# Expert routing rewritten: pairwise comparisons, unnormalised exponentials, ranks summed in PSUM, places in two halves

## Chip, cores and metric

The kernel runs on one core of one Trainium2 chip. The metric is the device time of one execution in microseconds; lower is better.

## What is computed

Two decoder layers over 512 tokens of width 1024. Layer 0 mixes tokens by sliding-window attention with sinks, layer 1 by forgetting attention. Each mixer is followed by a layer norm, a mixture of experts and another layer norm. The part that matters here is the router of the mixture of experts, which both layers share:

```python
def grouped_moe(h, w_router, b_router, w_gate, w_up, w_down):
    logits = (h2 @ w_router).astype(jnp.float32) + b_router.astype(jnp.float32)
    scores = jax.nn.softmax(logits, axis=-1)
    g = scores.reshape(T, N_GROUPS, EXPERTS_PER_GROUP)        # 4 groups of 4 experts
    group_score = jnp.sum(lax.top_k(g, TOP_K)[0], axis=-1)    # sum of the two best
    best = jnp.argmax(group_score, axis=-1)
    in_group = jax.nn.one_hot(best, N_GROUPS, dtype=jnp.bool_)[:, :, None]
    masked = jnp.where(in_group, g, -1.0).reshape(T, N_EXPERTS)
    top_vals, top_idx = lax.top_k(masked, TOP_K)              # two experts of that group
    gates = top_vals / jnp.sum(top_vals, axis=-1, keepdims=True)
    ...
    hg = jnp.einsum('td,edf->tef', h2, w_gate)
    hu = jnp.einsum('td,edf->tef', h2, w_up)
    act = jax.nn.silu(hg) * hu * gate_dense[:, :, None].astype(h2.dtype)
    y = jnp.einsum('tef,efd->td', act, w_down)
```

Each token uses two experts of one group, with gates that sum to 1.

## The kernel before

Every engine has a program written out by hand, with semaphores between them; there is no scheduler. Tokens lie in NT = 4 tiles of 128 on the partitions. The helper `link` puts a semaphore on a VectorE instruction and makes the next one wait for it, since a later instruction on the same engine may otherwise start before the result is written.

In a layer, the stages are: input projection, attention, output projection with the first norm (four token tiles, each followed by `route(t)`, the router's matmuls L648 into bank 7), the routing, the expert loop, the sum of each token's two expert rows with the second norm. The residual state goes to DRAM (`xd`) on ScalarE's queue as soon as a tile is normed (L909).

**The routing** (VectorE, L1248 to L1330) works on tiles of 128 partitions with 4 token tiles x 16 experts = 64 columns. It adds the bias and subtracts the maximum (L1251 to L1253), ScalarE takes the exponential (L913), and then VectorE

- sums and divides (L1255 to L1257);
- forms the six pair sums of every group, whose maximum is the group's score (L1259 to L1262);
- finds the best group, ties going to the first, through a maximum, an equality, a product with falling numbers `w4`, and a second maximum and equality (L1263 to L1268);
- masks the other groups (L1270 to L1273) and finds the best expert and the second in the same way with `w16` (the loop L1274 to L1282): one-hot tiles `oh1` and `oh2`;
- writes their sum `asn_b` in bf16 (L1283), which TensorE waits for;
- prepares `id_part`, one-hot times token number in fp16 (L1286), and the gates (L1287 to L1290);
- waits for the ranks. TensorE has multiplied `asn_b` by a strictly triangular matrix (`before_b`, L674: how many tokens earlier in the tile chose the expert) and by ones (L675: the tile's count). VectorE copies both from PSUM, forms running totals over the tiles and adds them (L1293 to L1297);
- picks each token's rank at its two experts (L1298, L1299) and compares it with the CAP = 96 places (`place_is`, L1300, 768 columns).

TensorE then multiplies `place_is` by `id_part` (L680, eight matmuls): the result is, for each expert and place, the token number. VectorE casts it into `row_ids` (L1303), and POOL gathers the rows of each expert from `xd` with an indirect DMA (L429), four experts ahead (experts 0 to 3 at once). What VectorE does after that (L1305 to L1329: overflow of an expert beyond 96 tokens, and `pos`, the place where each token's rows will be found) is needed at the end of the expert loop.

**The expert loop.** For expert e, TensorE turns the gathered rows (`turn_rows`, L687), ScalarE copies them as the high part (L925), VectorE forms the low part (L1336), and TensorE runs gate and up in three products per tile (L491 to L493). Meanwhile ScalarE and VectorE split the next expert's weights (L904, L1222). The down product is L713. SP loads the weights through a ring of four slots. The loads for experts 0 to 3 are issued from the end of the output projection on; from expert 4 on each waits for `gu_done` or `y_done` of the expert four back.

Of the kernel before, what the change touches and what calls it, by code (L numbers as in the profile page):

```python
# [48 lines left out]
def trunk(nc, x, ln_gain, ln_bias, swa_w_in, swa_sinks, swa_w_o, fox_w_in, fox_b_f, fox_w_o,  # L49
# [8 lines left out]
    with ctx:  # L58
# [77 lines left out]
        red = small(SM + 640, 10, NT)  # L136
        ids = small(SM + 684, OVF + 1)
# [4 lines left out]
        w4 = sb("w4", [P, NG])  # L142
        w16 = sb("w16", [P, NE])
# [105 lines left out]
        def _(eng):  # L249
# [33 lines left out]
            for l, (w_in, w_o) in enumerate(((swa_w_in[0], swa_w_o[0]), (fox_w_in[0], fox_w_o[0]))):  # L283
# [40 lines left out]
                eng.wait_ge(S(f"routed{l}"), 1)  # L324
# [18 lines left out]
        def _(eng):  # L343
# [16 lines left out]
            link(eng.iota(w4[:, :], [[-1, NG]], base=NG, channel_multiplier=0, allow_small_or_imprecise_dtypes=True))  # L360
            link(eng.iota(w16[:, :], [[-1, NE]], base=NE, channel_multiplier=0, allow_small_or_imprecise_dtypes=True))
# [104 lines left out]
        def _(eng):  # L466
# [16 lines left out]
            for l in range(DEPTH):  # L483
# [158 lines left out]
                def route(t):  # L642
# [7 lines left out]
                    mm.then_inc(S(f"logits{l}"), 1)  # L650
# [66 lines left out]
                def step(i, u, first=False, last=False):  # L717
# [5 lines left out]
                    if not first:  # L723
                        eng.wait_ge(S(f"h_ready{l}"), e)
                        turn_h((u - 1) % 2).then_inc(S(f"hT_done{l}"), 1)
# [7 lines left out]
                def down_of(e, b, use, loaded, reused):  # L733
                    eng.wait_ge(S(f"d_loaded{use % RING}"), loaded)
                    eng.wait_ge(S(f"hT_ready{l}"), e + 1)
                    if reused:
                        eng.wait_ge(S(f"y_act{l}"), e)
                        eng.wait_ge(S(f"y_dve{l}"), e)
# [12 lines left out]
                eng.wait_ge(S(f"h_ready{l}"), NE)  # L751
                turn_h(1).then_inc(S(f"hT_done{l}"), 1)
# [3 lines left out]
                with eng.If(n_ovf > 0):  # L756
                    eng.wait_ge(S(f"y_act{l}"), NE)
                    eng.wait_ge(S(f"y_dve{l}"), NE)
# [13 lines left out]
        def _(eng):  # L772
# [32 lines left out]
            for l in range(DEPTH):  # L805
# [111 lines left out]
                def store_rows(e, b):  # L917
                    eng.wait_ge(S(f"y_dve{l}"), e + 1)
                    eng.wait_ge(S(f"y_act{l}"), e + 1)
# [9 lines left out]
                def silu(e, b):  # L929
                    eng.wait_ge(S(f"gu_done{l}"), e + 1)  # L930
                    eng.activation(ssb[0:CAP, b, :], bank[2 + b][0:CAP, 0:F], ACT.Silu).then_inc(S(f"silu{l}"), 1)
# [528 lines left out]
```

## Time and profile before

| | us |
|---|---|
| median of 3 runs | 988.99 (987.59 to 992.05) |
| the profiled execution | 988.5 |
| its span in the profile | 986.6 |
| PE busy | 829.8 (84%) |
| VectorE busy | 547.7 (56%) |
| ScalarE busy | 383.9 (39%) |
| POOL busy | 136.1 (14%) |
| share of the chain that ended last: PE, DVE, DMA | 81%, 9%, 4% |

The profile is one execution, recorded by the hardware. "Span" is from its first to its last instruction; the execution's own time is 1.9 us longer. PE is TensorE's matmuls, PEld its weight loads, DVE VectorE, ACT ScalarE, POOL GpSimd, SP the engine that issues most DMAs. Busy shares are averages over stages with different limits, so what a change in one stage is worth has to be read in that stage.

### The profile page before, as it was taken

The page shows a single profiled execution, that of the slowest core. Times are in us where ns is not written, and L with a number is a line of the kernel's source. Part 1 is how long each engine was busy: PE and PEld are TensorE (multiplying, and loading weights), DVE is VectorE, ACT ScalarE, POOL GpSimd, SP SyncE. Part 2 cuts the span into 40 slices and gives each one's busy share as a digit, 9 for nine tenths or more (in the row PEclk, how much of TensorE's full clock was granted, in tenths as well). Part 3 has the DMA queues.
Part 4 walks back from the last instruction along what each step waited for, and adds up shares of the span by engine and source line. Part 5 has one row for each costly group of instructions (what it writes and reads, how often), then busy time and mean ns, then how long its engine had stood idle before and what let it go on. Part 6 is the DMA issues. An engine that isn't in the chain of part 4 may idle for free.

```text
span 986.6 us, 11641 instructions
## 1 busy us (share of the span) xinstructions
PE 829.8 (84%) x4140; PEld 601.7 (61%) x4140; DVE 547.7 (56%) x1086; ACT 383.9 (39%) x763; POOL 136.1 (14%) x153
## 2 busy tenths in 40 slices
PE   6999999981989999818999999999981889999910
PEld 4887777871546565417878877887861556556500
DVE  4534884556557676366332225664556556767437
ACT  4323884002455555231222226775001365555300
POOL 2000221121001000032000002221111100100033
PEclk9999999985899999959999999999985799999965
DMA  9942000149699998645062223111139599999144
GB/s 320 349 138 86 2 1 1 43 170 336 189 353 332 360 353 316 219 141 183 30 215 86 86 86 107 65 44 44 43 119 360 151 340 340 361 357 374 42 124 158
DMA packets 106851, 183.11 MB, mean 186 GB/s; under 512 B 6496, under 2 KB 72032, under 8 KB 106800
## 3 DMA queue, kind: packets, MB, share of 16 engines
q1 hardware_dynamic: 92864, 132.34, 39.7%
q0 software_dynamic: 9200, 33.33, 10.9%
q10 hardware_dynamic: 4736, 16.78, 4.5%
q8 instruction: 29, 0.48, 0.2%
q14 instruction: 22, 0.18, 0.1%
HBM read 159.60 MB, written 22.84 MB: 185 GB/s over the span
## 4 chain that ended last, share of the span: by engine, by line
PE 81%; DVE 9%; DMA 4%; issue 3%; POOL 2%; ACT 1%; POOLq 0%; DVEq 0%; SPq 0%; ACTq 0%
PE bank L491 16%; PE bank L492 16%; PE bank L493 16%; PE bank L713 12%; PE bank L613 5%; PE bank L579 4%; PE bank L596 3%; PE bank L687 2%; PE bank L477 2%; DMA arena<-xd,row_ids 1%; PE bank L648 1%; POOL veps L387 1%; DVE xres L1042 1%; DMA arena<-ys,pos 1%; PE bank L621 1%
## 5 line engine op out<-in xcount | busy, mean ns | idle before, releaser
L1222 DVE TENSOR_TENSOR low<-ring,gu_high 128x1024 fp32r<-128x1024 f32 x128 | 151.2, 1221 | 50.6 <-ACT gu_high L904 50.6
L904 ACT CAST gu_high<-ring 128x1024 fp32r<-128x1024 f32 x128 | 127.7, 1049 | 16.8 <-DVE arena L1353 16.8
L713 PE MATMUL bank<-ring,arena 128*96 128x512 f32 x256 | 119.8, 611 | 11.3 <-issue 9.2
L491 PE MATMUL bank<-gu_high,rows_high 128*96 128x512 f32 x256 | 115.4, 451 | 8.2 <-DVE rows_low L1336 8.2
L492 PE MATMUL bank<-low,rows_high 128*96 128x512 f32 x256 | 103.6, 405 | 0.0
L493 PE MATMUL bank<-gu_high,rows_low 128*96 128x512 f32 x256 | 103.0, 402 | 0.0
L713 PEld LDWEIGHTS bank<-ring,arena 128*96 128x96 f32 x256 | 40.1, 167 | 67.7 <-issue 67.3
L852 ACT ACTIVATE arena<-arena,nmax 128x256 f32<-128x256 f32 (+3 forms) x128 | 66.8, 522 | 30.8 <-DVE nmax L1153 20.0
L491 PE MATMUL bank<-high,x_high 128*128 128x512 f32 x160 | 66.2, 414 | 10.3 <-DVE low L1048 5.1
L414 POOL TENSOR_TENSOR low<-ring,high 128x512 fp32r<-128x512 f32 x32 | 40.6, 1269 | 231.1 <-ACT high L872 231.1
L613 PE MATMUL bank<-arena 128*128 128x64 f32 x544 | 68.1, 269 | 0.2 <-ACT arena L866 0.2
L613 PEld LDWEIGHTS bank<-arena 128*128 128x128 f32 x544 | 65.8, 192 | 0.5 <-ACT arena L866 0.5
L429 POOL DMA_INDIRECT arena<-xd,row_ids x32 | 30.2, 944 | 258.2 <-PE bank L687 220.0
L492 PE MATMUL bank<-low,x_high 128*128 128x512 f32 x160 | 64.7, 404 | 0.0
L493 PE MATMUL bank<-high,xlow 128*128 128x512 f32 x160 | 64.6, 404 | 0.0
L491 PEld LDWEIGHTS bank<-gu_high,rows_high 128*96 128x96 f32 x256 | 42.9, 167 | 33.3 <-DVE rows_low L1336 9.1
L492 PEld LDWEIGHTS bank<-low,rows_high 128*96 128x96 f32 x256 | 42.7, 167 | 23.7 <-issue 7.9
L493 PEld LDWEIGHTS bank<-gu_high,rows_low 128*96 128x96 f32 x256 | 42.7, 167 | 19.2 <-issue 0.9
L491 PE MATMUL bank<-high,attn_high 128*128 128x512 f32 x128 | 51.5, 402 | 0.0
L493 PE MATMUL bank<-high,attn_low 128*128 128x512 f32 x128 | 51.3, 401 | 0.0
L491 PE MATMUL bank<-x_high,wsplit 128*128 128x512 f32 x128 | 50.8, 397 | 0.0
L492 PE MATMUL bank<-xlow,wsplit 128*128 128x512 f32 x128 | 50.8, 397 | 0.0
(207 smaller groups left out, 1399.2 us busy)
## 6 DMA issues: line engine op xcount, KB each, us to landing
ring<-in_w_gate SPq DMA_DIRECT2D x32, 1024.0 KB, 12.3
ring<-in_w_up SPq DMA_DIRECT2D x32, 1024.0 KB, 14.4
ring<-in_w_down SPq DMA_DIRECT2D x32, 1024.0 KB, 12.7
ys<-arena ACTq DMA_DIRECT2D x32, 384.0 KB
ring<-in_fox_w_in SPq DMA_DIRECT2D x6, 2048.0 KB, 10.7
ring<-in_swa_w_in SPq DMA_DIRECT2D x3, 2048.0 KB, 8.8
ring<-in_swa_w_o SPq DMA_DIRECT2D x2, 2048.0 KB, 17.4
xd<-xres ACTq DMA_DIRECT2D x8, 512.0 KB, 2.6
```

The costliest lines, as they stand in the source:

```text
L414: eng.tensor_tensor(low, w, high, ALU.subtract).then_inc(S(f"out_low{l}"), 1)
L429: eng.indirect_dma_start(xe[0:CAP, e % RING, :], None, xd, bass.IndirectOffsetOnAxis(ap=row_ids[:, e:e + 1], axis=0)).then_inc(S(f"xe_in{l ...
L491: eng.matmul(out, ah, wh, start=(c == 0), stop=False)
L492: eng.matmul(out, ah, wl, start=False, stop=False)
L493: return eng.matmul(out, al, wh, start=False, stop=(c == KC - 1))
L579: mm = eng.matmul(s_bank(s, half)[:, 0:nk], QT[r, hp, n * P:(n + 1) * P], KT[r, kp, k0 * P:k1 * P], start=True, stop=(l == 0))
L596: mm = eng.transpose(bank[3 + half][:, i * P:(i + 1) * P], sp[:, 2 * (s % 2) + half, i * P:(i + 1) * P], ident[:, :])
L613: mm = eng.matmul(bank[5 + hp % 2][:, at:at + HD], pT[:, half, i * P:(i + 1) * P], (V0 if l == 0 else V)[:, k0 + i, v:v + HD], start=(i == ...
L713: mm = eng.matmul(bank[5 + half][0:CAP, :], hT[:, b, c, :], w[:, c, half * BLK:(half + 1) * BLK], start=(c == 0), stop=(c == FC - 1))
L852: eng.activation(p, p, ACT.Exp, bias=nmax[:, hp % 2, n, half:half + 1], scale=-1.0, accum_out=rsum[:, hp % 2, n, half:half + 1]).then_inc( ...
L904: eng.copy(gu_high[u % 2][:, part, :], slot_in(use)[:, part, :]).then_inc(S("gu_high"), 1)
L1222: eng.tensor_tensor(lows[use % RING][:, part, :], slot_in(use)[:, part, :], gu_high[u % 2][:, part, :], ALU.subtract).then_inc(S("gu_low"), 1)
```

## The change

- The exponentials are no longer divided by their sum. The gates are a ratio, and all comparisons are inside a token, so the common factor drops out.
- The best group: each group's score is compared with the score of each group (16 differences per token), a difference must reach `lead`, which is 0 or 1e-30 depending on which of the two comes first, and the minimum over the row says whether a group wins against all (`gk`).
- The scores of the best group's four experts are collected into `best` (product with `gk` in the turned order, then a sum). Again each is compared with each, and the number of wins (4: first, 3: second) gives `top`, `won` and from them `asn_b`, `oh1` and `oh2`.
- TensorE sums the ranks over the tiles in PSUM: tile t of bank 2 gets `before_b` times its own tile and `ones_b` times each earlier tile (10 matmuls of 16 columns), and the total of each expert goes to bank 6 (4 matmuls). VectorE's running totals go away; it reads the ranks in PSUM directly.
- `place_is` is written in two halves of 384 columns, and TensorE's wait for it is split the same way.
- The gates and the copies of ranks and counts move behind `row_ids`. One product of the gates, `won` times `best`, stands between `place_is` and the wait for `ids_done`.
- On POOL at the start, the iotas of `w4` and `w16` become a memset and a select for `lead`.
- Many semaphores that had one name per layer (`routed`, `logits`, `hT_done`, `h_ready`, `hT_ready`, `y_act`, `y_dve`, `silu`) now have one for both layers, with the wait counts raised by NE or NT in layer 1; who waits for whom stays.

The core of the diff:

```diff
                 eng.wait_ge(S("assigned"), l + 1)
-                eng.matmul(bank[2][:, 0:NT * NE], before_b[:, :], asn_b[:, :], start=True, stop=True)
-                eng.matmul(bank[6][:, 0:NT * NE], ones_b[:, :], asn_b[:, :], start=True, stop=True).then_inc(S("ranked"), 1)
-
-                eng.wait_ge(S("places_ready"), l + 1)
+                for t in range(NT):
+                    for u in range(t + 1):
+                        mm = eng.matmul(bank[2][:, t * NE:(t + 1) * NE], before_b[:, :] if u == t else ones_b[:, :],
+                                        asn_b[:, u * NE:(u + 1) * NE], start=(u == 0), stop=(u == t))
+                mm.then_inc(S("ranked"), 1)
+                for t in range(NT):
+                    mm = eng.matmul(bank[6][:, 0:NE], ones_b[:, :], asn_b[:, t * NE:(t + 1) * NE], start=(t == 0), stop=(t == NT - 1))
+                mm.then_inc(S("counted"), 1)
+
                 for k in range(TOPK):
+                    eng.wait_ge(S("places_ready"), TOPK * l + k + 1)
                     for t in range(NT):
...
                 eng.wait_ge(S("expd"), l + 1)
-                link(eng.tensor_reduce(sm, pr, X, ALU.add))
-                link(eng.reciprocal(rs, sm))
-                link(eng.tensor_tensor(pr, pr, over(rs, NE), ALU.mult))
...
                 link(eng.tensor_reduce(gs, pair, X, ALU.max))
-                link(eng.tensor_reduce(gm, gs, X, ALU.max))
-                link(eng.tensor_tensor(gk, gs, over(gm, NG), ALU.is_equal))
-                link(eng.tensor_tensor(gk, gk, tiles(w4[:, :]), ALU.mult))
-                link(eng.tensor_reduce(kb, gk, X, ALU.max))
-                link(eng.tensor_tensor(gk, gk, over(kb, NG), ALU.is_equal))
...
-                for v, kk, oh in ((v1, k1, oh1), (v2, k2, oh2)):
-                    link(eng.tensor_reduce(v, msk, X, ALU.max))
-                    link(eng.tensor_tensor(tmp, msk, over(v, NE), ALU.is_equal))
-                    link(eng.tensor_tensor(tmp, tmp, tiles(w16[:, :]), ALU.mult))
-                    link(eng.tensor_reduce(kk, tmp, X, ALU.max))
-                    link(eng.tensor_tensor(oh, tmp, over(kk, NE), ALU.is_equal))
...
+                link(eng.tensor_tensor(square, *against(gs), ALU.subtract))
+                link(eng.tensor_tensor(square, square, leads, ALU.is_ge))
+                link(eng.tensor_reduce(gk, square, X, ALU.min))
+
+                by_place = tmp.rearrange("p t (e g) -> p t e g", g=NG)
+                link(eng.tensor_tensor(by_place, prg.rearrange("p t g e -> p t e g"), against(gk)[1], ALU.mult))
+                link(eng.tensor_reduce(best, by_place, X, ALU.add))
+
+                link(eng.tensor_tensor(square, *against(best), ALU.subtract))
+                link(eng.tensor_tensor(square, square, leads, ALU.is_ge))
+                link(eng.tensor_reduce(wins, square, X, ALU.add))
+                link(eng.tensor_scalar(top, wins, EPG - 1.5, None, ALU.is_ge))
+                eng.tensor_tensor(asn_b[:, :].rearrange("p (t g e) -> p t g e", t=NT, g=NG), against(top)[1], against(gk)[0], ALU.mult).then_inc(S("assigned"), 1)
+                eng.tensor_scalar(won[:, 0, :, :], wins, float(EPG), None, ALU.is_equal)
+                link(eng.tensor_scalar(won[:, 1, :, :], wins, EPG - 1.0, None, ALU.is_equal))
+                for k, oh in enumerate((oh1, oh2)):
+                    ins = eng.tensor_tensor(oh.rearrange("p t (g e) -> p t g e", g=NG), against(won[:, k, :, :])[1], against(gk)[0], ALU.mult)
+                link(ins)
...
+                eng.wait_ge(S("ranked"), l + 1)
+                lranks = bank[2][:, 0:NT * NE].rearrange("p (t e) -> p t e", t=NT)
+                link(eng.tensor_tensor(lp12, oh12, lranks.unsqueeze(1).to_broadcast([P, 2, NT, NE]), ALU.mult))
+                link(eng.tensor_reduce(rank[:, :, :], lp12, X, ALU.add))
+                for k in range(TOPK):
+                    eng.tensor_tensor(place_is[:, k, :, :], places[:, :].unsqueeze(1).to_broadcast([P, NT, CAP]),
+                                      rank[:, k, :].unsqueeze(2).to_broadcast([P, NT, CAP]), ALU.is_equal).then_inc(S("places_ready"), 1)
+                eng.tensor_tensor(won, won, best.unsqueeze(1).to_broadcast([P, 2, NT, EPG]), ALU.mult).then_inc(S("dve_won"), 1)
+                eng.wait_ge(S("ids_done"), l + 1)
+                eng.tensor_copy(row_ids[:, :], bank[5][0:CAP, 0:NE]).then_inc(S("ids_ready"), 1)
+                eng.wait_ge(S("dve_won"), l + 1)
+                eng.tensor_reduce(v1, won[:, 0, :, :], X, ALU.add)
+                link(eng.tensor_reduce(v2, won[:, 1, :, :], X, ALU.add))
```

The order of instructions is the order in the code. VectorE, layer 0, from the reduction of the pair sums; in the kernel before the piece shown ends at the first maximum of the expert search, 12 instructions ahead of `asn_b` (`arena` holds all the small tiles, `w` is `w4` or `w16`):

```order
L1262 TENSOR_REDUCE arena<-arena 128x16
L1263 TENSOR_REDUCE arena<-arena 128x4
L1265 TENSOR_TENSOR arena<-arena 128x16
L1266 TENSOR_TENSOR arena<-arena,w 128x16
L1267 TENSOR_REDUCE arena<-arena 128x4
L1268 TENSOR_TENSOR arena<-arena 128x16
L1270 TENSOR_SCALAR arena<-arena 128x16
L1272 TENSOR_TENSOR arena<-arena 128x64
L1273 TENSOR_TENSOR arena<-arena 128x64
L1275 TENSOR_REDUCE arena<-arena 128x4
```

The same place with the change, up to `asn_b`:

```order
L1270 TENSOR_REDUCE arena<-arena 128x16
L1278 TENSOR_TENSOR arena<-arena 128x64
L1279 TENSOR_TENSOR arena<-arena,lead 128x64
L1280 TENSOR_REDUCE arena<-arena 128x16
L1283 TENSOR_TENSOR arena<-arena 128x64
L1284 TENSOR_REDUCE arena<-arena 128x16
L1286 TENSOR_TENSOR arena<-arena 128x64
L1287 TENSOR_TENSOR arena<-arena,lead 128x64
L1288 TENSOR_REDUCE arena<-arena 128x16
L1289 TENSOR_SCALAR arena<-arena 128x16
L1290 TENSOR_TENSOR asn_b<-arena 128x64
```

The search for the best group has become three instructions, and `asn_b` follows after five more on the four collected scores and one threshold.

VectorE, layer 0, from the arrival of the ranks to the cast of the row numbers, before:

```order
L1293 COPY arena<-bank 128x64
L1294 COPY arena<-bank 128x64
L1296 TENSOR_TENSOR arena<-arena 128x16 x3
L1297 TENSOR_TENSOR arena<-arena 128x48
L1298 TENSOR_TENSOR arena<-arena 128x128
L1299 TENSOR_REDUCE arena<-arena 128x8
L1300 TENSOR_TENSOR place_is<-places,arena 128x768
L1303 CAST row_ids<-bank 96x16
```

With the change, from the instruction behind `asn_b` (`bank` is the rank tile in PSUM):

```order
L1291 TENSOR_SCALAR arena<-arena 128x16
L1292 TENSOR_SCALAR arena<-arena 128x16
L1294 TENSOR_TENSOR arena<-arena 128x64 x2
L1298 TENSOR_TENSOR id_part<-arena,tok_id 128x128
L1302 TENSOR_TENSOR arena<-arena,bank 128x128
L1303 TENSOR_REDUCE arena<-arena 128x8
L1305 TENSOR_TENSOR place_is<-places,arena 128x384 x2
L1307 TENSOR_TENSOR arena<-arena 128x32
L1309 CAST row_ids<-bank 96x16
```

The copies and running totals ahead of the masked ranks are gone, the one-hot tiles come ahead of them instead, and the places are two instructions.

TensorE, layer 0, from the ranks to the turning of expert 0's rows, before:

```order
L648 MATMUL bank7<-wr,xT 128x16 x8
L674 MATMUL bank2<-asn_b,before_b 128x64
L675 MATMUL bank6<-asn_b,ones_b 128x64
L680 MATMUL bank5<-id_part_59,place_is_58 96x16 x8
L687 MATMUL bank0<-ident,arena 128x96 x4
```

With the change:

```order
L681 MATMUL bank2<-asn_b,before_b 128x16
L681 MATMUL bank2<-asn_b,ones_b 128x16
L681 MATMUL bank2<-asn_b,before_b 128x16
L681 MATMUL bank2<-asn_b,ones_b 128x16 x2
L681 MATMUL bank2<-asn_b,before_b 128x16
L681 MATMUL bank2<-asn_b,ones_b 128x16 x3
L681 MATMUL bank2<-asn_b,before_b 128x16
L685 MATMUL bank6<-asn_b,ones_b 128x16 x4
L691 MATMUL bank5<-id_part_59,place_is_58 96x16 x8
L698 MATMUL bank0<-ident,arena 128x96 x4
```

One matmul of 64 columns has become ten of 16 ahead of the signal `ranked`, and the counts come behind it.

## Rows read from the trace of the kernel before

**Rows 1.** The page, chain that ended last, shares of the span by engine

```profile
PE 81%; DVE 9%; DMA 4%; issue 3%; POOL 2%; ACT 1%; POOLq 0%; DVEq 0%; SPq 0%; ACTq 0%
```

**Rows 2.** Chain in order of time, both layers' first gather: start us, us, what

```profile
235.31 6.25 DMA arena<-xd,row_ids
...
241.60 1.55 PE bank L687 x8
...
244.14 1.03 DVE rows_low L1336 x2
...
756.36 8.06 DMA arena<-xd,row_ids
```

**Rows 3.** Timeline of VectorE, layer 0, routing: start us, us, line, shapes

```profile
223.19 0.22 DVE L1255 TENSOR_REDUCE arena<-arena 128x4 f32<-128x64 f32 x1 [0.32 <-ACT arena L913]
...
223.92 0.21 DVE L1259 TENSOR_TENSOR arena<-arena 128x48 f32<-128x48 f32 x1
...
224.36 0.25 DVE L1262 TENSOR_REDUCE arena<-arena 128x16 f32<-128x96 f32 x1
224.65 0.17 DVE L1263 TENSOR_REDUCE arena<-arena 128x4 f32<-128x16 f32 x1
...
225.68 0.17 DVE L1270 TENSOR_SCALAR arena<-arena 128x16 f32<-128x16 f32 x1
225.89 0.22 DVE L1272 TENSOR_TENSOR arena<-arena 128x64 f32<-128x64 f32 x1
226.15 0.22 DVE L1273 TENSOR_TENSOR arena<-arena 128x64 f32<-128x64 f32 x1
...
229.47 0.23 DVE L1283 TENSOR_TENSOR asn_b<-arena 128x64 bf16<-128x64 f32 x1
229.61 0.28 DVE L1286 TENSOR_TENSOR id_part<-arena,tok_id 128x128 f16<-128x128 f32 x1
229.81 0.15 DVE L1287 TENSOR_TENSOR arena<-arena 128x4 f32<-128x4 f32 x1
...
230.49 0.22 DVE L1293 COPY arena<-bank 128x64 f32<-128x64 f32 x1
...
231.75 0.29 DVE L1298 TENSOR_TENSOR arena<-arena 128x128 f32<-128x128 f32 x1
...
232.39 0.96 DVE L1300 TENSOR_TENSOR place_is<-places,arena 128x768 f16<-128x768 f32 x1
234.25 0.17 DVE L1303 CAST row_ids<-bank 96x16 uint32<-96x16 f32 x1 [0.90 <-PE bank L680]
...
239.79 0.17 DVE L1329 CAST ovf_id<-arena 1x11 int32<-1x11 f32 x1
```

**Rows 4.** Timeline of VectorE, layer 1, routing

```profile
744.29 0.22 DVE L1255 TENSOR_REDUCE arena<-arena 128x4 f32<-128x64 f32 x1 [0.32 <-ACT arena L913]
...
755.36 0.17 DVE L1303 CAST row_ids<-bank 96x16 uint32<-96x16 f32 x1 [0.90 <-PE bank L680]
```

**Rows 5.** Timeline of TensorE in the routing; last row: line L680, min/median/max ns

```profile
229.75 0.24 PE L674 MATMUL bank<-asn_b,before_b 128*128 128x64 bf16 x1 [7.66 <-DVE asn_b L1283]
229.76 0.12 PEld L675 LDWEIGHTS bank<-asn_b,ones_b 128*128 128x128 bf16 x1
...
233.40 0.81 PE L680 MATMUL bank<-id_part,place_is 128*96 128x16 f16 x8 [3.36 <-DVE place_is L1300]
...
L680 PE MATMUL bank<-id_part,place_is x16: 227/228/248, 233.4 to 755.1; 128*96 128x16 f16 x16
```

**Rows 6.** Windows, all engines, layer 0: busy us, PE clock, DMA share, GB/s

```profile
225.00:230.00 5.00, 0.25 (x2) 0.13 (x2) 4.32 (x22) 0.98 (x2) 0.00 (x0) 0.50 1.06 388
...
240.00:245.00 5.00, 1.54 (x8) 1.25 (x8) 0.86 (x2) 1.80 (x3) 0.91 (x1) 0.50 0.92 234
245.00:250.00 5.00, 4.78 (x12) 3.22 (x13) 3.57 (x4) 0.34 (x1) 0.00 (x0) 0.52 0.29 83
```

**Rows 7.** Line L429, the gathers: issue to landing, those the view could pair

```profile
DMA to landing us min/median/max: 6.7/7.8/9.1
```

More of the change, by code:

```diff
@@ L136, in trunk @@
         red = small(SM + 640, 10, NT)
+        best = small(SM + 816, NT, EPG)
+        wins = small(SM + 832, NT, EPG)
+        won = small(SM + 848, 2, NT, EPG)
+        top = small(SM + 880, NT, EPG)
         ids = small(SM + 684, OVF + 1)
@@ L359, in _ @@
                                    base=0, pattern=[[-1, P]], channel_multiplier=1))
-            link(eng.iota(w4[:, :], [[-1, NG]], base=NG, channel_multiplier=0, allow_small_or_imprecise_dtypes=True))
-            link(eng.iota(w16[:, :], [[-1, NE]], base=NE, channel_multiplier=0, allow_small_or_imprecise_dtypes=True))
+            link(eng.memset(lead[:, :, :], 0.0))
+            link(eng.affine_select(out=lead[:, :, :], in_=lead[:, :, :], compare_op=ALU.is_ge, fill=1e-30,
+                                   base=0, pattern=[[-1, NG], [1, EPG]], channel_multiplier=0))
             link(eng.iota(e_cap[:, :], [[CAP, NE]], base=0, channel_multiplier=0, allow_small_or_imprecise_dtypes=True))
@@ L1246, in tiles @@
                     return a.unsqueeze(1).to_broadcast([P, NT, a.shape[1]])
-                mx, sm, rs, gm, kb, v1, k1, v2, k2 = (red[:, k, :] for k in range(9))
-                eng.wait_ge(S(f"logits{l}"), NT)
+                mx, sm, rs, v1, v2 = (red[:, k, :] for k in range(5))
+                eng.wait_ge(S("logits"), NT + NT * l)
                 lps = bank[7][:, 0:NT * NE].rearrange("p (t e) -> p t e", t=NT)
@@ L1290, in _ @@
                 link(eng.tensor_tensor(gates[:, :, 1], v2, rs, ALU.mult))
-                eng.wait_ge(S("ranked"), l + 1)
-                eng.tensor_copy(tmp, bank[2][:, 0:NT * NE].rearrange("p (t e) -> p t e", t=NT))
-                link(eng.tensor_copy(tot, bank[6][:, 0:NT * NE].rearrange("p (t e) -> p t e", t=NT)))
-                for t in range(1, NT):
-                    link(eng.tensor_tensor(tot[:, t, :], tot[:, t, :], tot[:, t - 1, :], ALU.add))
-                link(eng.tensor_tensor(tmp[:, 1:NT, :], tmp[:, 1:NT, :], tot[:, 0:NT - 1, :], ALU.add))
-                link(eng.tensor_tensor(lp12, oh12, tmp.unsqueeze(1).to_broadcast([P, 2, NT, NE]), ALU.mult))
-                link(eng.tensor_reduce(rank[:, :, :], lp12, X, ALU.add))
-                eng.tensor_tensor(place_is[:, :, :, :], places[:, :].unsqueeze(1).unsqueeze(1).to_broadcast([P, 2, NT, CAP]),
-                                  rank[:, :, :].unsqueeze(3).to_broadcast([P, 2, NT, CAP]), ALU.is_equal).then_inc(S("places_ready"), 1)
-                eng.wait_ge(S("ids_done"), l + 1)
-                eng.tensor_copy(row_ids[:, :], bank[5][0:CAP, 0:NE]).then_inc(S("ids_ready"), 1)
+                eng.wait_ge(S("counted"), l + 1)
+                eng.tensor_copy(tmp, lranks)
+                link(eng.tensor_copy(tot[:, NT - 1, :], bank[6][:, 0:NE]))
                 cnt = tot[:, NT - 1, :]
```

59 lines of the change are left out of this document (27 added, 32 removed).

## The prediction

> **What bounds the kernel now.** I read the page's chain of waits first. It puts 81% of the span on TensorE and 9% on VectorE [rows 1], so I looked for the places where VectorE is on the chain. The chain in order of time shows them: in each layer, between the router's logits and the first expert, TensorE has next to nothing to do and waits for a serial piece of VectorE work, then for the gather of expert 0's rows [rows 2]. In layer 0 the gather starts at 235.31 and takes 6.25 us; in layer 1 it starts at 756.36 and takes 8.06 us. Behind it follow the turning of the rows (241.60), VectorE's low parts (244.14) and the experts.
>
> The timeline of VectorE shows the serial piece [rows 3]: from L1255 (223.19) to the start of the row numbers' cast L1303 (234.25) are 11.06 us, nearly all of it instructions of 0.15 to 0.3 us, each waiting for the one before. Layer 1 has the same piece: 744.29 to 755.36, 11.07 us [rows 4]. Nothing hides it, because gather, TensorE and ScalarE's L925 all stand behind it. So a microsecond off this piece is a microsecond off the span, twice, unless the gather gives it back. TensorE's part is small: the two rank matmuls wait for L1283 and start at 229.75, the eight L680 take 0.81 us [rows 5].
>
> **What the change does, per layer.** I cost by distance from start to start, since that holds the link's wait too.
>
> *Up to asn_b.* Before: 223.19 to 229.47, 6.28 us. Now the first instruction after the exponentials is the pair sum. The three pair sums up to L1262 take 0.44 (223.92 to 224.36), the reduction of pairs 0.29 (224.36 to 224.65). Then come eight 64-wide linked steps (difference, comparison, reduction, masked product, reduction, difference, comparison, count); such a step takes 0.26 (225.89 to 226.15). A 16-wide scalar step (top) takes 0.21 (225.68 to 225.89). Sum 0.44 + 0.29 + 8 x 0.26 + 0.21 = 3.02, so 3.26 less. No row before reads a 64-wide tile in the turned order that by_place uses; between 0.21 and 0.29 for each of the eight steps the sum is 2.6 to 3.3. I take 0.26, because L1272 already reads with broadcast strides at that price.
>
> *asn_b to the masked ranks.* Before: 229.47 to 231.75 (L1298), 2.28 us, with the gates' arithmetic, two copies out of PSUM and the running totals in it. Now VectorE needs 0.14 (229.47 to 229.61, the step of an instruction that the next need not wait for), 0.14 and 0.21 for won, 0.14 and 0.26 for the two one-hot tiles, 0.20 for id_part (229.61 to 229.81): 1.09. But it then waits for ten matmuls where there was one on that path. TensorE starts 0.28 after asn_b's start (229.75 less 229.47). L680 gives 0.81 for eight with 96-wide weights and 0.23 for one, so 0.083 for each further one; with 128-wide weights 0.083 x 128 / 96 = 0.11. That makes 0.28 + 9 x 0.11 + 0.24 + 0.02 = 1.53 us, so the matmuls are late, not VectorE. Ends: 1.28 (0.083 each) and 1.65 (0.12, the weight load of L675). Gain 0.75. The four "counted" matmuls behind (0.44) end before place_is is there. The masked ranks now read PSUM themselves. The 64-wide copy out of PSUM, L1293, took 0.22 us and 64-wide operations inside SBUF 0.22 to 0.23 [rows 3], so I add nothing. The Trainium skill ("VectorE: DVE Perf Modes", the section on the TRN2 errata) gives PSUM sources a fixed part 62 cycles longer, which would be 0.06 us per layer; the rows do not show it.
>
> *The places.* L1298 to L1300 stays at 0.64. From L1300 to L1303 were 1.86: 0.96 for 768 columns, eight matmuls 0.81, 0.09 for signals. With (0.96 - 0.28) / 640 = 1.06 ns a column (L1286 has 128 columns at 0.28), a half of 384 takes 0.55 and lets the second start after 0.47 (asn_b, 0.23 long, let the next start after 0.14, some 0.08 ahead of its end). The second half ends at 1.02, four matmuls then take 0.81 - 4 x 0.083 = 0.48, with signals 1.59. Gain 0.27; the ends are 0 (the halves overlap with nothing) and 0.4.
>
> *Sum per layer*: 3.26 + 0.75 + 0.27 = 4.28 us, ends 3.6 and 4.8.
>
> *What moves behind the row numbers.* won times best (one 32-wide step, 0.2) stands ahead of the wait for ids_done, while TensorE still works at the second half. Behind L1303 go the gates and two copies, some 1.4 us. VectorE was done 5.7 us after L1303 began (234.25 to 239.96) and is next wanted at 244.14 [rows 2, 3], so 7.1 us of work lie under 9.9 us. Cost nothing; if the gather took over 2.8 us less, this tail would be what is late next. The two iotas become a memset and a select on POOL at the start, long before use. The merged semaphores add some additions on registers in layer 1's loops on PE, ACT and DVE, in front of waits; the matmuls of the loop show no gap at the ones that are there. Nothing.
>
> **What the gather gives back.** Its issue moves from 235.31 to about 231.0. There the DMA engines are fuller: at 225 to 230 their share is 1.06 with 388 GB/s, at 240 to 245 it is 0.92 with 234 GB/s, and at 245 to 250 only 0.29 [rows 6]. The weight loads of experts 0 to 3 run until about then. Layer 0's 6.25 us had the end of this burst; issued earlier, it has the full stream, as the gathers in the expert loop do. Those land in 6.7 to 9.1 us, median 7.8 [rows 7]. I take 7.8 for both layers: +1.55 in layer 0, -0.26 in layer 1, together +1.3.
>
> **Sum.** 988.5 (the profiled execution's own time; the median of the runs is 989.0) - 2 x 4.28 + 1.3 = **981.2 us**, 0.8% less. The experts and the second layer shift with it: their loads are released by TensorE's own progress.
>
> **Rivals.**
> 1. *The gather ends with the burst whenever it is issued.* For it: both first gathers landed (241.56, 764.42) near the end of the burst, and the rate drops behind. Then the 4.28 us are spent waiting: **988.5**. Against it: in the loop gathers land in 7.8 us under a stream that does not end. The Trainium skill ("DMA: Bandwidth & Descriptors", Queues, rings and completion order) says that a DMA's completion is written only after all earlier writes of that DMA engine, over all its queues; by that rule the gather would wait for the weights already in flight, and the loop's 7.8 us bound how much. Chance 0.09.
> 2. *The gather is not slowed at all.* 6.25 us in both layers: 988.5 - 8.6 - 1.8 = **978.1**. For it: layer 0's 6.25 was under a nearly full stream too (0.92 at 240 to 245). Against: layer 1, the same place, took 8.06. Chance 0.10.
> 3. *Slower: the four gathers share.* POOL issues gathers 0 to 3 one after another. If rows of all four go out side by side under the full stream, gather 0 completes only with the last of them, at the end of the burst: by 245 in layer 0 [rows 6], by 766.1 in layer 1, whose routing stands 521.1 later [rows 3, 4]. That is 3.4 and 1.7 later than now, **993.6**. It decides from a landing of 10.5 us on (6.25 + 4.28), where the gain of layer 0 is gone; no landing that the view gives is above 9.1 [rows 7]. Chance 0.03.
>
> A last uncertainty is TensorE's clock. It was at the lower level (1.2 GHz, 0.50) while TensorE waited and on the mean still at 0.52 at 245 to 250, with TensorE busy again for 4.78 of 5 us [rows 6]. How long the low stretch lasts after the restart can come out otherwise when the start shifts: I allow 1 us in all, either way.
>
> **How the numbers follow.** The forecast's case (landings of 7.1 to 9.1, mean near 7.8) has 0.78. Its ends: -9.6 - 1.8 - 1 gives 976.1 and -7.2 + 3.9 (both at 9.1) + 1 gives 986.2; I give **976.5 to 986.0**, which leaves out rivals 1 and 3 and little else, some 15%. Half a percent, about what a measurement of this kernel can tell, is 4.9 us: faster means under 984.1, slower over 993.9. Of the forecast's case 0.07 lies above 984.1, so faster 0.71 + 0.10 = 0.81; same 0.07 + 0.09 + 0.01 = 0.17; slower 0.02, the part of rival 3 that a lost microsecond or two of clock pushes over.
>
> **What would show it.** The distance from ScalarE's exponential to the row numbers' cast should be 6.5 to 7.3 us instead of 11.06, in both layers. asn_b should start about 3.0 after the first pair sum, and the masked ranks about 1.5 after asn_b, with VectorE waiting for the rank matmuls. The gather of expert 0 should take 7 to 9 us in layer 0. Wrong would be: a gather over 9 us (rival 1 or 3), VectorE late for L1336, or turned reads well over 0.26 us a step.

## Result and profile after

The kernel with the change takes 982.72 us in the median of 7 runs (980.65 to 983.39), the kernel before 990.42 us (7 runs, 987.59 to 993.27): ratio 0.9918, 95% interval 0.99 to 0.9936. The forecast was 981.2 us in a range of 976.5 to 986.0. The profiled execution of the changed kernel took 981.84 us, that of the kernel before 988.5.

The page of the changed kernel, its span and the shares of its chain:

```profile
span 980.1 us, 11701 instructions
...
PE 82%; DVE 8%; DMA 4%; issue 3%; POOL 2%; ACT 1%; POOLq 0%; SPq 0%; DVEq 0%; ACTq 0%
```

The span is 6.5 us shorter than before (986.6), VectorE's share of the chain one point smaller [rows 1]. VectorE in layer 0's routing and, last two rows, in layer 1's (start, duration, instruction):

```profile
223.02 0.21 DVE L1267 TENSOR_TENSOR arena<-arena 128x48 f32<-128x48 f32 x1 [0.32 <-ACT arena L924]
...
223.47 0.25 DVE L1270 TENSOR_REDUCE arena<-arena 128x16 f32<-128x96 f32 x1
223.75 0.22 DVE L1278 TENSOR_TENSOR arena<-arena 128x64 f32<-128x64 f32 x1
...
224.52 0.26 DVE L1283 TENSOR_TENSOR arena<-arena 128x64 f32<-128x64 f32 x1
224.82 0.22 DVE L1284 TENSOR_REDUCE arena<-arena 128x16 f32<-128x64 f32 x1
...
226.05 0.22 DVE L1290 TENSOR_TENSOR asn_b<-arena 128x64 bf16<-128x64 f32 x1
...
227.08 0.28 DVE L1302 TENSOR_TENSOR arena<-arena,bank 128x128 f32<-128x128 f32 x1
...
227.72 1.03 DVE L1305 TENSOR_TENSOR place_is<-places,arena 128x384 f16<-128x384 f32 x2
...
229.32 0.17 DVE L1309 CAST row_ids<-bank 96x16 uint32<-96x16 f32 x1 [0.48 <-PE bank L691]
...
236.10 0.16 DVE L1345 CAST ovf_id<-arena 1x11 int32<-1x11 f32 x1
...
740.91 0.21 DVE L1267 TENSOR_TENSOR arena<-arena 128x48 f32<-128x48 f32 x1 [0.32 <-ACT arena L924]
...
747.22 0.17 DVE L1309 CAST row_ids<-bank 96x16 uint32<-96x16 f32 x1 [0.48 <-PE bank L691]
```

From the first instruction after the exponentials to the row numbers' cast: 223.02 to 229.32, 6.30 us, where 11.06 stood [rows 3]; in layer 1 740.91 to 747.22, 6.31 us [rows 4]. That is 4.76 us less, twice; I had 4.28. TensorE in the same stretch, with `[idle before]` at the ends:

```profile
226.33 0.19 PE L681 MATMUL bank<-asn_b,before_b 128*128 128x16 bf16 x1 [4.41 <-DVE asn_b L1290]
...
226.62 0.25 PE L685 MATMUL bank<-asn_b,ones_b 128*128 128x16 bf16 x4
228.33 0.96 PE L691 MATMUL bank<-id_part,place_is 128*96 128x16 f16 x8 [1.45 <-DVE place_is L1305]
```

The rank matmuls start 0.28 us after `asn_b` and those ahead of `ranked` are spread over 0.3 us; `place_is` is what TensorE waits for. The chain from the gathers on, both layers:

```profile
230.39 7.99 DMA arena<-xd,row_ids
...
238.42 1.55 PE bank L698 x8
...
240.96 1.03 DVE rows_low L1352 x2
...
748.23 7.41 DMA arena<-xd,row_ids
```

Against [rows 2]: the gather in layer 0 takes 7.99 us instead of 6.25, the one in layer 1 7.41 instead of 8.06. Together 1.09 us of the gain is given back there. VectorE's work behind the row numbers ended at 236.26, 4.7 us before it was wanted at 240.96.

How the 6.5 us come about, each figure the difference of the same event in the two traces (after less before):

| event | after | before | difference |
|---|---|---|---|
| layer 0, first instruction after the exponentials | 223.02 | 223.19 | -0.17 |
| row numbers cast | 229.32 | 234.25 | -4.93 |
| expert 0's first gate/up matmul | 242.03 | 245.22 | -3.19 |
| layer 1, first instruction after the exponentials | 740.91 | 744.29 | -3.38 |
| row numbers cast | 747.22 | 755.36 | -8.14 |
| expert 0's first gate/up matmul | 759.29 | 768.09 | -8.80 |
| last down product | 928.66 | 936.33 | -7.67 |
| end of span | 980.1 | 986.6 | -6.5 |

By its restart, the first gate/up matmul of expert 0, layer 1 had won 8.8 us, of which 2.3 are gone at the end. Windows of 10 us from that restart, before and after (columns as in [rows 6]):

```profile
768.09:778.09 10.00, 8.26 (x32) 5.66 (x32) 4.58 (x6) 2.21 (x6) 0.90 (x1) 0.80 0.20 59
```

```profile
759.29:769.29 10.00, 9.05 (x32) 6.14 (x32) 3.79 (x5) 1.42 (x5) 0.67 (x1) 0.72 0.59 157
```

TensorE's mean granted clock is 0.72 instead of 0.80. In the single matmuls the lower level (one matmul every 0.43 us, 1.2 GHz) lasted 5.67 us after the restart instead of 3.95; in layer 0 it lasted 4.27 instead of 4.72. The expert loop of layer 1 is 1.1 us longer, and 0.8 of that is there already when the rows of expert 1 are turned (8.23 us behind the restart instead of 7.44). Another 1.0 us is the last store of expert rows, in the chain of the kernel before and of this one:

```profile
940.73 2.99 DMA ys<-arena
```

```profile
933.06 3.96 DMA ys<-arena
```

### The profile page after: what moved, and what is told of

Read it like the earlier page. It is cut to its first block, busy times and chain, and to the rows that moved or that the text cites. A ratio compares the mean times of both kernels' runs of the same rounds, so it can differ in the third digit from the quotient of the medians.

```text
span 980.1 us, 11701 instructions
## 1 busy us (share of the span) xinstructions
PE 831.0 (85%) x4164; PEld 602.4 (61%) x4164; DVE 542.4 (55%) x1066; ACT 384.2 (39%) x763; POOL 136.4 (14%) x153
## 4 chain that ended last, share of the span: by engine, by line
PE 82%; DVE 8%; DMA 4%; issue 3%; POOL 2%; ACT 1%; POOLq 0%; SPq 0%; DVEq 0%; ACTq 0%
PE bank L496 17%; PE bank L497 16%; PE bank L498 16%; PE bank L724 12%; PE bank L618 5%; PE bank L584 4%; PE bank L601 3%; PE bank L698 2%; PE bank L482 2%; DMA arena<-xd,row_ids 2%; PE bank L653 1%; DMA arena<-ys,pos 1%; POOL veps L392 1%; DVE xres L1053 1%; DVE stats L1038 1%
```

## Experiments

"Behind the exponentials" is below the distance from VectorE's first instruction after them to the cast of the row numbers, 11.06 us before and 6.30 after the change. Timed kernels come with a ratio to the kernel before in the same session.

**Only the comparisons.** The changed kernel with two rank matmuls and totals on VectorE, `place_is` in one piece, and the gates ahead of the ranks:

```diff
-                for t in range(NT):
-                    for u in range(t + 1):
-                        mm = eng.matmul(bank[2][:, t * NE:(t + 1) * NE], before_b[:, :] if u == t else ones_b[:, :],
...
+                eng.matmul(bank[2][:, 0:NT * NE], before_b[:, :], asn_b[:, :], start=True, stop=True)
+                eng.matmul(bank[6][:, 0:NT * NE], ones_b[:, :], asn_b[:, :], start=True, stop=True).then_inc(S("ranked"), 1)
...
+                link(eng.tensor_tensor(won, won, best.unsqueeze(1).to_broadcast([P, 2, NT, EPG]), ALU.mult))
+                eng.tensor_reduce(v1, won[:, 0, :, :], X, ALU.add)
+                link(eng.tensor_reduce(v2, won[:, 1, :, :], X, ALU.add))
...
+                eng.tensor_tensor(place_is[:, :, :, :], places[:, :].unsqueeze(1).unsqueeze(1).to_broadcast([P, 2, NT, CAP]),
...
```

> Only the comparisons and the unnormalised exponentials; ranks, places and the position of the gates as before. My theory (VectorE's steps are worth their length, twice): from the first instruction after the exponentials to the cast of the row numbers 8.8 us instead of 11.06 (3.0 to asn_b, then 2.0 with the gates in it, 1.26 of copies and totals, 0.64, 1.86), and the gather lands after 7 to 8 us, so 4.5 us less minus about 1 = 987 against 990.4. Rival (the gather ends with the burst of weight loads whenever it is issued): the same 8.8 us, but a landing longer by the 2.3 us won in each layer, and the time of before, 990.4.

Measured: 989.45 us, ratio 0.9981 (0.9967 to 0.9994), so only 2 us less than before. Behind the exponentials 9.02 us (222.85 to 231.87), 2.04 less. Up to `asn_b` it is 3.2 us less, but from there to the masked ranks it takes 3.47 us instead of 2.28, because the one-hot tiles, which stood ahead of `asn_b` before, now come behind it with `won`, and the gates have seven instructions instead of four. The chain:

```profile
232.93 8.69 DMA arena<-xd,row_ids
...
753.80 8.42 DMA arena<-xd,row_ids
```

The gather in layer 0 was issued 2.38 us earlier than before (232.93 against 235.31) and landed at 241.62, where it had landed at 241.56, so all of it was given back. In layer 1 it took 8.42 against 8.06 and gave back 0.36 of 2.07. The rival wanted both layers and the time of before, and falls. Nor does layer 0 show its mechanism, a gather that ends with the burst. In four of the kernels below that gather is issued 1.2 to 2.1 us earlier, takes 8.60 to 8.77 us there too, and lands earlier (239.46 to 240.50). In the changed kernel it landed at 238.38, while the last weight load of the burst, issued at 227.97, took 20.3 us, until 248.3. So layer 0 gave back all it had because the gather of the kernel before had 6.25 us, and one that is issued a little earlier has some 8.7.

**Ranks as before**, all else changed: the two rank matmuls above, and on VectorE

```diff
-                link(eng.tensor_tensor(lp12, oh12, lranks.unsqueeze(1).to_broadcast([P, 2, NT, NE]), ALU.mult))
+                eng.tensor_copy(tmp, bank[2][:, 0:NT * NE].rearrange("p (t e) -> p t e", t=NT))
+                link(eng.tensor_copy(tot, bank[6][:, 0:NT * NE].rearrange("p (t e) -> p t e", t=NT)))
+                for t in range(1, NT):
+                    link(eng.tensor_tensor(tot[:, t, :], tot[:, t, :], tot[:, t - 1, :], ALU.add))
+                link(eng.tensor_tensor(tmp[:, 1:NT, :], tmp[:, 1:NT, :], tot[:, 0:NT - 1, :], ALU.add))
+                link(eng.tensor_tensor(lp12, oh12, tmp.unsqueeze(1).to_broadcast([P, 2, NT, NE]), ALU.mult))
...
```

> The changed kernel with the ranks as before: two matmuls of 64 columns, both copies out of PSUM and the running totals. In the changed kernel the masked ranks start 1.03 us after asn_b. Theory now: this part is worth the 1.26 us of copies and totals in full, because ten narrow matmuls of 128-wide bf16 weights take only some 0.3 us; masked ranks 2.3 us after asn_b, span of the routing 7.56 instead of 6.30 us, 2 to 3 us more in all. Rival (my prediction's sizing): ten matmuls cost 0.5 us of it, so the part is worth 0.75 us per layer and the masked ranks come 1.8 us after asn_b.

VectorE in layer 0:

```profile
226.17 0.23 DVE L1284 TENSOR_TENSOR asn_b<-arena 128x64 bf16<-128x64 f32 x1
...
228.45 0.29 DVE L1300 TENSOR_TENSOR arena<-arena 128x128 f32<-128x128 f32 x1
```

`asn_b` to the masked ranks is 2.28 us against 1.03 in the changed kernel: 1.25, as the theory had it, not my 0.75. One run gave 988.5 us. The gathers took 8.60 and 8.46 us here, 1.7 us more in all than in the changed kernel. With 2 x 1.25 that makes 4.2 of the 5.8 us between the two. The trace places another 1.7 us where the two kernels are the same, between layer 0's last down product and layer 1's routing. Most of it is in the output projection of layer 1, whose first eight matmuls come 0.43 us apart (679.95 to 683.44), the lower clock level, and 0.23 us apart in the changed kernel. Seven of the twelve variants have such a slow projection in their traces, the kernel before and the changed kernel do not.

**`place_is` in one piece**, all else changed:

```diff
+                eng.wait_ge(S("places_ready"), l + 1)
                 for k in range(TOPK):
-                    eng.wait_ge(S("places_ready"), TOPK * l + k + 1)
...
-                for k in range(TOPK):
-                    eng.tensor_tensor(place_is[:, k, :, :], places[:, :].unsqueeze(1).to_broadcast([P, NT, CAP]),
...
+                eng.tensor_tensor(place_is[:, :, :, :], places[:, :].unsqueeze(1).unsqueeze(1).to_broadcast([P, 2, NT, CAP]),
+                                  rank[:, :, :].unsqueeze(3).to_broadcast([P, 2, NT, CAP]), ALU.is_equal).then_inc(S("places_ready"), 1)
```

> The changed kernel with place_is in one piece. Theory: place_is to row_ids 1.86 us instead of 1.60, so 0.26 us more per layer, 0.5 in all, below what the times can tell. Rival (the halves hide nothing, since TensorE's second half waits for VectorE anyway): 1.60 to 1.65 us here too.

```profile
227.17 0.96 DVE L1304 TENSOR_TENSOR place_is<-places,arena 128x768 f16<-128x768 f32 x1
...
229.03 0.17 DVE L1308 CAST row_ids<-bank 96x16 uint32<-96x16 f32 x1 [0.80 <-PE bank L691]
```

1.86 us from `place_is` to the row numbers against 1.60: the halves are worth 0.26 us per layer. The one run took 984.4 us, which says nothing about half a microsecond.

**The gates ahead of the ranks**, all else changed:

```diff
+                link(eng.tensor_tensor(won, won, best.unsqueeze(1).to_broadcast([P, 2, NT, EPG]), ALU.mult))
+                eng.tensor_reduce(v1, won[:, 0, :, :], X, ALU.add)
+                link(eng.tensor_reduce(v2, won[:, 1, :, :], X, ALU.add))
+                link(eng.tensor_tensor(sm, v1, v2, ALU.add))
+                link(eng.reciprocal(rs, sm))
+                eng.tensor_tensor(gates[:, :, 0], v1, rs, ALU.mult)
+                link(eng.tensor_tensor(gates[:, :, 1], v2, rs, ALU.mult))

                 eng.wait_ge(S("ranked"), l + 1)
...
```

> The changed kernel with the gates' arithmetic back ahead of the wait for the ranks (seven small instructions). Theory: rank matmuls are done long before VectorE gets there (1.03 us behind asn_b), so VectorE's 1.0 us of gates is paid in full: masked ranks 2.0 us behind asn_b, 1.0 us more per layer. Rival (the gates hide under the wait for the ten matmuls, as my sizing of 1.53 us had it): masked ranks at 1.5 us, half of it hidden.

```profile
226.21 0.23 DVE L1290 TENSOR_TENSOR asn_b<-arena 128x64 bf16<-128x64 f32 x1
...
228.42 0.29 DVE L1309 TENSOR_TENSOR arena<-arena,bank 128x128 f32<-128x128 f32 x1
```

From `asn_b` to the masked ranks 2.21 us instead of 1.03: 1.18 us, nothing of it hidden. Moving the gates behind the row numbers is thus nearly as large a part of the gain as the ranks in PSUM. The four parts add up to the whole: 2.04 for the comparisons, 1.25 for the ranks, 1.18 for the gates and 0.26 for the halves make 4.73 of the 4.76 us. The one run took 988.84 us; 2 x 1.18 and gathers that were 1.9 us longer (8.77 and 8.50) make 4.2 of its distance of 6.1, and this trace too has the slow projection in layer 1 and 1.7 us more between the same two places.

**Loads held.** To see what makes the gather slow, SP holds what is left of the burst:

```diff
                     if u >= OUT_BLOCKS:
                         load_gate_up(k, l, u, S(f"w_loaded{k % RING}"))
+                    if u == OUT_BLOCKS:
+                        eng.wait_ge(S(f"xe_in{l}0"), 16)
                     load_down(k, l, u, S(f"d_loaded{k % RING}"))
```

> The changed kernel, but SP holds the down weights of expert 2 and all loads of expert 3 until the gather of expert 0 has landed. Theory (the gather is slow because it shares the DMA engines with the burst of weight loads): it lands in 3 to 4 us instead of 8.0 and 7.4, expert 0 starts some 4 us earlier in each layer, 974 to 976 us. Rival 1 (the gather's own work, index reading and descriptors on POOL, is the 6 to 8 us): landing unchanged, 982. Rival 2 (held loads come late): landing 3 to 4 us, but ScalarE waits for the weights of expert 3 at its split, and the time is 982 or above.

Measured: 977.44 us, ratio 0.986 (0.9839 to 0.9881). The chain, and windows of layer 0 around the issue:

```profile
230.06 5.28 DMA arena<-xd,row_ids
...
747.77 4.56 DMA arena<-xd,row_ids
```

```profile
228.00:230.00 2.00, 0.96 (x8) 0.79 (x8) 1.42 (x9) 0.00 (x0) 0.00 (x0) 0.50 0.00 0
...
232.00:234.00 2.00, 0.00 (x0) 0.00 (x0) 1.76 (x8) 0.00 (x0) 1.39 (x3) 0.50 0.72 207
```

At the issue the DMA engines are idle, and the gathers take 5.28 and 4.56 us instead of 7.99 and 7.41: 5.6 us less. The median is 5.3 us below the 982.7 of the changed kernel; the two profiled executions are only 3.7 apart, because this one has the slow projection (1.7 us). Rivals 1 and 2 fall: the stream of weights is what made it 8 us, and the held loads came early enough. But 3 to 4 us was too low.

**Gathers staged**, without and with the held loads:

```diff
                 for e in range(NE):
+                    if e == 1:
+                        eng.wait_ge(S(f"xe_in{l}0"), 16)
                     if e >= RING:
```

> The changed kernel with the gathers of experts 1 to 3 issued after that of expert 0 has landed, the weight loads not held. Theory (the stream of weights, not the following gathers, makes it 8 us): 7 to 8 us, time 981 to 983. Rival (the four gathers share, rival 3 of the prediction): 5 to 6 us, 978 to 980.

> As the kernel with the held loads, and POOL issues the gathers of experts 1 to 3 only when that of expert 0 has landed. With held loads alone gather 0 took 5.28 and 4.56 us though the DMA engines were idle when it was issued. Theory (the four gathers share the engines): 3 to 3.7 us, some 3 us less in all than with the held loads alone, 975 against 977.4. Rival (one gather alone takes 4.6 to 5.3 us): no change in landing, and gathers 1 to 3 come later, into the held weight loads: 977 to 979.

Staged alone: 981.32 us, ratio 0.9902 (0.9887 to 0.9917), landings of 7.82 and 7.34 us. The following gathers are not what slows the first; rival 3 of the prediction falls. Staged and held: 976.08 us, ratio 0.9854 (0.9835 to 0.9872); its interval does not part it from held alone. The chains of the two, staged alone first:

```profile
230.53 7.82 DMA arena<-xd,row_ids
...
748.85 7.34 DMA arena<-xd,row_ids
```

```profile
230.42 4.76 DMA arena<-xd,row_ids
...
745.19 4.17 DMA arena<-xd,row_ids
```

4.76 and 4.17 us is what one gather of 96 rows took on idle engines. That is 0.5 and 0.4 less than with the three others behind it, but in the next run, of the kernel before, a gather with the three others behind it takes 4.72 and 4.66, so what they add is not shown. My 3 to 3.7 us was wrong.

**The kernel before with held loads**, the same edit.

> The kernel before with the held loads. Theory (the part that the gather gave back came from the stream of weight loads): both kernels' first gathers now take 4.6 to 5.3 us, and the change is worth its full 2 x 4.76 = 9.5 us: 977.4 + 9.5 = 987 (the kernel before 990.4). Rival (what was given back came from elsewhere): the distance stays at 7.7 us, 985.

Measured: 985.68 us, ratio 0.9944 (0.9924 to 0.9964). Its gathers:

```profile
235.05 4.72 DMA arena<-xd,row_ids
...
755.68 4.66 DMA arena<-xd,row_ids
```

They take 4.7 us each, against 5.28 and 4.56 with the change, and held loads alone take 0.56% off the kernel before. Held against held the medians are 8.2 us apart, without holding 7.7; the intervals are too wide to tell 7.7 from 9.5. In the traces expert 0 starts, counted from VectorE's first instruction after the exponentials, 4.2 and 4.8 us earlier with the change when loads are held, 3.0 and 5.4 when not: 9.0 against 8.4. The direction is the theory's, the size is not settled.

**Wide weights for the row numbers:**

```diff
-                        mm = eng.matmul(bank[5][0:CAP, 0:NE], place_is[:, k, t, :], id_part[:, k, t, :],
+                        mm = eng.matmul(bank[5][:, 0:NE], place_w[:, k, t * CAP:t * CAP + P], id_part[:, k, t, :],
...
```

> The changed kernel with the stationary operand of the row number matmuls 128 columns wide instead of 96 (32 padding columns of zeros behind each half; the output rows they feed are not read). Theory: 96-wide weights load at 0.083 us each, 128-wide bf16 or fp16 weights at some 0.03, as the ten rank matmuls showed; so the last four matmuls take 0.25 instead of 0.48 us and place_is to row_ids goes from 1.60 to some 1.4 us. Rival (the rank matmuls were fast because of their operands' values or order, not their width): 1.60 stays, or 1.7 for the wider weights.

TensorE in layer 0 with wide weights:

```profile
227.71 0.27 PE L691 MATMUL bank<-id_part,place_w 128*128 128x16 f16 x4 [1.45 <-DVE place_w L1306]
228.18 0.28 PE L691 MATMUL bank<-id_part,place_w 128*128 128x16 f16 x4 [0.20 <-DVE place_w L1306]
```

Four matmuls with 128-wide fp16 weights take 0.27 us with their end, and the row numbers are cast 1.40 us after `place_is` (227.09 to 228.49) instead of 1.60. VectorE waits 0.27 us for the last of them ahead of the cast, 0.48 with 96 columns. One weight load takes 0.11 us (median of 16) instead of 0.19, although it has more columns, so the width decides and not the operands' values or order. The one run took 983.86 us, which again says nothing about half a microsecond.

**TensorE kept busy during the gather:**

```diff
                 mm.then_inc(S("ids_done"), 1)
+                for t in range(11):
+                    eng.matmul(bank[4][:, 0:256], ident[:, :], xres[:, t % NT, 0:256], start=True, stop=True)
```

> The changed kernel with eleven extra fp32 matmuls of 256 columns on TensorE while it waits for the gather (results not used). Theory (part of what is left is TensorE's lower clock level after the wait): the clock is granted in full before the rows land, the turning of the rows takes 0.8 instead of 1.55 us, and the 4.3 and 5.7 us of slow matmuls after the restart lose 2 and 2.6 us; 4 to 6 us less in all, 977 to 979. Rival (the clock falls again in the gap of 1 to 2 us that is left, or in the gap for rows_low): 982 as the changed kernel.

Measured: 982.29 us, ratio 0.9917 (0.9902 to 0.9932): no gain. TensorE (the trace has each of these fp32 matmuls twice, so eleven stand as x22):

```profile
229.59 6.86 PE L695 MATMUL bank<-xres,ident 128*128 128x256 f32 x22
239.50 0.92 PE L700 MATMUL bank<-ident,arena 96*128 96x96 f32 x8 [3.04 <-DMA arena<-xd,row_ids]
242.50 0.74 PE L496 MATMUL bank<-gu_high,rows_high 128*96 128x512 f32 x1 [2.08 <-DVE rows_low L1354]
243.04 0.63 PE L497 MATMUL bank<-low,rows_high 128*96 128x512 f32 x1
```

The rows are turned in 0.92 us instead of 1.54, so the clock had risen, though TensorE had been idle for 3.04 us. After a further wait of 2.08 us the first matmul is at 0.74 with 0.63 behind it, the lower level. The rival was right.

**The same, with four more such matmuls in each gap of 2 us around expert 0:**

```diff
...
                 turn_rows(0).then_inc(S(f"xeT_done{l}"), 1)
+                idle(4)
                 step(0, 0, first=True)
+                idle(4)
                 step(0, 1)
```

> The changed kernel with the eleven extra matmuls of the earlier run and four more in each gap of 2 us around expert 0. There the clock had risen before the rows landed and fell again by the restart, with no gain (0.9917 against 0.9918). Theory (what TensorE does in the gaps decides): both low stretches go, 982.7 less 2 x (0.6 + 2.2 + 1.6) = 974 to 976. Rival: the clock falls after the first expert all the same, 980 to 982.

Measured: 976.95 us, ratio 0.9851 (0.9824 to 0.9877). TensorE in layer 1:

```profile
757.24 0.88 PE L704 MATMUL bank<-ident,arena 96*128 96x96 f32 x8 [1.63 <-DMA arena<-xd,row_ids]
757.96 1.92 PE L700 MATMUL bank<-xres,ident 128*128 128x256 f32 x8
760.20 0.47 PE L496 MATMUL bank<-gu_high,rows_high 128*96 128x512 f32 x1 [0.32 <-DVE rows_low L1360]
...
765.80 0.82 PE L704 MATMUL bank<-ident,arena 96*128 96x96 f32 x8
```

Here expert 0's gate and up products run at the full clock from the first matmul on, and the turning of expert 1's rows comes 5.60 us after them (760.20 to 765.80); in the changed kernel it was 8.23. In layer 0 of this profile TensorE had stood idle for 3.00 us ahead of the rows; their turning still ran at the full clock (0.89 us), but the four added matmuls behind it took 3.52 us instead of 1.92, and the mean granted clock was 0.66 at 240 to 245. So the clock fell there after all, and rose again during these four; expert 0's products run at the full level from the second on (one every 0.23 us from 244.17).

**All of it**: held loads, staged gathers, wide weights, thirty short matmuls behind the logits, six during the gather, four in each gap:

```diff
                 route(NT - 1)
+                for t in range(30):
+                    eng.matmul(bank[4][:, 0:P], ones_b[:, :], ident_b[:, :], start=True, stop=True)
...
```

> Held loads, staged gathers, wide weights, and TensorE kept busy with matmuls whose results are not used: thirty short ones behind the logits, six while it waits for the gather, four each in the two gaps of 2 us around expert 0. Theory: 976.1 less 2 x 0.2 (wide), less 2 x 0.7 (turning at the full clock), less 2 x (2.2 + 1.6) for the two low stretches around expert 0: 967 to 969. Rival (the clock falls anyway, or the extra matmuls make TensorE late): 975 to 977.

Measured: 969.45 us (5 runs, 968.43 to 971.98), ratio 0.9792 (0.9772 to 0.9812). That is half a microsecond above the theory's range, and faster than both kernels. What the thirty short matmuls add to it is not shown, since no run leaves only them out. TensorE in layer 0:

```profile
222.34 3.36 PE L682 MATMUL bank<-ident_b,ones_b 128*128 128x128 bf16 x30
...
229.51 4.89 PE L701 MATMUL bank<-xres,ident 128*128 128x256 f32 x12
235.47 0.88 PE L710 MATMUL bank<-ident,arena 96*128 96x96 f32 x8 [1.07 <-DMA arena<-xd,row_ids]
236.19 1.92 PE L706 MATMUL bank<-xres,ident 128*128 128x256 f32 x8
238.43 0.47 PE L500 MATMUL bank<-gu_high,rows_high 128*96 128x512 f32 x1 [0.32 <-DVE rows_low L1367]
```

## Why the prediction was right, step by step

- *Up to `asn_b`*: 3.02 us expected, 3.03 measured (223.02 to 226.05). Counting links from start to start was enough. The turned read (L1283) took 0.30 from start to start instead of 0.26, one hundredth over the bound that I gave for a step, and was the only step to do so.
- *`asn_b` to the masked ranks*: 1.53 expected, 1.03 measured. This is the term that was mis-sized. I took the ten matmuls at the pace of L680, 0.083 us each, and scaled it up with the width of the weights to 0.11; they came at 0.03 each (ten from 226.33 to 226.62), so VectorE, for which I had worked out 1.09 us, was the later of the two and did not wait. The lower bound of 1.28 was also too high, and for this term alone the distance behind the exponentials came out at 6.30 us, below the 6.5 to 7.3 that I had named as the sign. The Trainium skill ("TensorE: Matmul & The Clock Gate", Weight-path perf modes) says that fast weight load is on when the number of weights is 128 and the type is not fp32; the rank matmuls and the wide variant agree with it, and I had not put that rule against the row that I scaled.
- *PSUM read*: 0.28 us for the 128-wide masked ranks out of PSUM, 0.29 before from SBUF. The fixed part 62 cycles longer that the Trainium skill states for PSUM sources ("VectorE: DVE Perf Modes", the section on the TRN2 errata) is not seen here either.
- *Places*: 1.59 expected, 1.60 measured, 1.86 with the halves undone.
- *The gather*: 7.8 expected for both, 7.99 and 7.41 measured; given back 1.09 us, expected 1.3. The reason stated (the burst of loads) was shown by holding the loads, which brings the first gather to 4.7 us in the kernel before and 5.28 and 4.56 in the changed one.
- *Covered work*: the gates and copies behind the row numbers cost nothing, as expected. As the held kernels bring the rows 3 us sooner, VectorE's end comes closer to being wanted: with everything together it ends at 236.60, and its next work starts at 237.35.
- *The clock and the end*: I allowed 1 us either way. Layer 1 lost 1.1 and layer 0 won 0.4; a further 1.0 was lost to a store, which I had not thought of.

The two errors nearly cancel: 0.5 us per layer more won in the ranks, 1.7 us in all less at the end. So the profiled executions are 6.7 us apart, where I had 7.3; that this is so near is partly luck. The median came out 1.5 us above the forecast, but I had subtracted from 988.5, and the kernel before has a median of 990.42 over seven runs: the medians are 7.7 us apart, and from that base my sum gives 983.1. In the range, the lower end of 976.1 takes 1.8 us off for the gathers, which are rival 2's landings of 6.25; my own case, from 7.1 us on, takes off only 0.1 and ends at 977.8. Rival 1 is borne out by no run: with the comparisons alone layer 0's gather landed when it had before, but its 8.69 us are what it took in four other kernels that issued it earlier and had it earlier.

## What to carry to other kernels

A serial chain of small instructions between two stages of the main engine is worth its length, so take out of it whatever nobody behind it needs yet; moving seven small instructions of the gates gave nearly as much as the ranks' new arithmetic. Then look at the transfer behind the chain: if it meets a burst of prefetches, let the burst wait for it. And where TensorE runs at its lower clock level after a wait, work whose result is not used can keep the level up: here that was worth some 6 us, about as much as the loads that were held.

## What the runs showed of the hardware that I had not expected

- Weights of 128 columns in bf16 or fp16 loaded much faster than fp16 weights of 96 columns: at the lower clock level (0.50) ten matmuls of 16 columns came 0.03 us apart, with 96-wide weights 0.083.
- The first gather (96 rows of 4 KB) took 4.1 to 5.3 us from issue to landing on idle DMA engines, in eight cases over four kernels, and 7.3 to 8.8 us with the stream of weight loads running, in nineteen cases over ten kernels. Only the kernel before, in layer 0, had 6.25. In kernels with the same routing layer 0's took 7.82 to 8.68, so half a microsecond of it is scatter.
- The lower clock level lasted between 3.0 and 6.0 us after the same restart, in 22 cases over the eleven kernels without added TensorE work. Together with the stretch at the lower level in layer 1's output projection, which seven of the fourteen traces have (1.7 us in the three that are set against the changed kernel above), a difference of one or two microseconds between two kernels of this kind can come from the clock alone.
